# Sparse attention of a two-model kernel: seven program blocks turned into one pipeline over pairs of heads

## The reference, cut to what matters

```python
s_c = einsum('bqgrd,bngd->bgrqn', q_blk, ck) * scale      # 15 compressed blocks
p_c = softmax(where(valid_c, s_c, NEG_INF)) * valid_c
o_c = einsum('bgrqn,bngd->bqgrd', p_c, cv)
...                                                       # o_s: chosen blocks, o_w: window of 512
out = g[..., 0:1] * o_c + g[..., 1:2] * o_s + g[..., 2:3] * o_w
```

## Time and profile before

| | us |
|---|---|
| median of 3 runs | 2824.45 (2823.25 to 2824.95) |
| the profiled execution | 2822.43 |
| its span | 2820.7 |
| TensorE, VectorE, ScalarE, GpSimd busy | 2485.3, 1855.9, 1334.9, 204.7 |
| mean granted TensorE clock, share of full | 0.91 |
| of it from `nsa`'s start to its end (1713.0 to 1849.4) | 136.4, granted clock 0.51 |

### The profile page before, as it was taken

How to read it: one execution, slowest core, us unless ns; L and a number is a source line. 1 busy time by engine, 2 the same in 40 slices (tenths; PEclk the granted TensorE clock), 3 DMA queues, 4 the chain that set the end, 5 groups by cost and what they waited for, 6 DMA issues and landing times. The chain is left out here.

```text
span 2820.7 us, 45360 instructions
## 1 busy us (share of the span) xinstructions
PE 2485.3 (88%) x17186; PEld 2233.7 (79%) x17186; DVE 1855.9 (66%) x3132; ACT 1334.9 (47%) x2140; POOL 204.7 (7%) x181
## 2 busy tenths in 40 slices
PE   7888999899978899795389985937899999999998
PEld 5877897789877789794389974626899999999997
DVE  3645555555564555656755552665899999999897
ACT  2343433443344344422144431303677777777776
POOL 0500000000013000071000032000000000000000
PEclk9999999999989999895589985558999999999999
DMA  8604554445531345340045440002799999999995
GB/s 322 253 16 182 214 215 151 165 174 215 194 107 44 132 172 191 126 150 0 0 150 187 172 169 15 1 0 83 287 344 328 342 343 327 341 343 333 329 344 219
DMA packets 82041, 541.75 MB, mean 192 GB/s; under 512 B 9328, under 2 KB 9776, under 8 KB 33840
## 3 DMA queue, kind: packets, MB, share of 16 engines
q1 hardware_dynamic: 79184, 529.57, 50.9%
q10 hardware_dynamic: 2656, 9.40, 0.9%
HBM read 537.88 MB, written 1.05 MB: 191 GB/s over the span
## 5 line engine op out<-in xcount | busy, mean ns | idle before, releaser
L843 PE MATMUL bank<-w_hi,src_hi 128*128 128x256 f32 x2304 | 671.8, 292 | 15.3 <-DVE src_lo L614 4.4
L2471 DVE TENSOR_TENSOR w_lo<-ring,w_hi 128x1024 fp32r<-128x1024 f32 x528 | 637.7, 1221 | 61.3 <-ACT w_hi L2407 41.8
L844 PE MATMUL bank<-w_lo,src_hi 128*128 128x256 f32 x2304 | 653.1, 283 | 0.0
L845 PE MATMUL bank<-w_hi,src_lo 128*128 128x256 f32 x2304 | 652.3, 283 | 0.0
L843 PEld LDWEIGHTS bank<-w_hi,src_hi 128*128 128x128 f32 x2304 | 441.3, 192 | 39.2 <-issue 30.4
L844 PEld LDWEIGHTS bank<-w_lo,src_hi 128*128 128x128 f32 x2304 | 442.0, 192 | 12.1 <-issue 6.7
L845 PEld LDWEIGHTS bank<-w_hi,src_lo 128*128 128x128 f32 x2304 | 442.1, 192 | 0.0
L843 PE MATMUL bank<-src_hi,w_hi 128*128 128x256 f32 x1472 | 426.8, 290 | 12.7 <-DVE w_lo L1150 8.9
L1150 DVE TENSOR_TENSOR w_lo<-ring,w_hi 128x1024 fp32r<-128x1024 f32 x264 | 322.8, 1223 | 169.5 <-ACT w_hi L1087 169.3
L844 PE MATMUL bank<-src_lo,w_hi 128*128 128x256 f32 x1472 | 421.9, 287 | 0.0
L845 PE MATMUL bank<-src_hi,w_lo 128*128 128x256 f32 x1472 | 421.5, 286 | 0.0
(11 more groups left out here) (349 smaller groups left out, 3076.5 us busy)
## 6 DMA issues: line engine op xcount, KB each, us to landing
ring<-in_moe SPq DMA_DIRECT2D x176, 1024.0 KB, 7.2
ring<-in_ffn SPq DMA_DIRECT2D x66, 1536.0 KB, 6.5
ring<-in_moe SPq DMA_DIRECT2D x176, 512.0 KB, 6.8
ring<-in_ffn_ev SPq DMA_DIRECT2D x22, 1536.0 KB, 6.6
oT<-in_w_ada SPq DMA_DIRECT2D x20, 1024.0 KB, 5.4
big<-in_w_ada SPq DMA_DIRECT2D x20, 1024.0 KB, 8.4
ring<-in_w_in SPq DMA_DIRECT2D x18, 1024.0 KB, 6.3
ring<-in_w_out SPq DMA_DIRECT2D x12, 1024.0 KB, 4.9
```

The source lines that it names most:

```text
L843: pe.matmul(out, ah, bh, start=start and i == 0, stop=False, skip_group_check=True)
L844: pe.matmul(out, ah, bl, start=False, stop=False, skip_group_check=True)
L845: mm = pe.matmul(out, al, bh, start=False, stop=stop and i == n - 1, skip_group_check=True)
L2471: dve.tensor_tensor(wl, piece, wh.bitcast(F32), ALU.subtract).then_inc(p.w_lo[kind].sem, 1)
```

## The change

`nsa_compress` goes, and `nsa` becomes a single block with one list for each engine. The helpers `turn`, `attention`, `head_norm` are no longer used there.

- Heads are reordered on the host (0, 4, 1, 5, ...), so that 128 neighbouring columns hold one head of each group. A transpose of 128x128 then gives a pair, and keys and values of both groups lie on both halves of the partitions too. `w1`, `w2` and the position columns are stored twice, on partitions 0 to 63 and 64 to 127.
- Compression: each group has its own half of the array's rows and of its output partitions: 64 products of 64x64 with 64x15 for each kind.
- Eight units: pair m (0 to 3), branch w (0 or 1). A unit holds both heads and both token tiles: 384 key columns a head. GpSimd builds the values with a column of ones. Gates are multiplied into the inverse sums.
- The compressed branch is laid as steps between the units (`compressed_step`): block-diagonal keys and values give all heads' scores in 8 products and the output of a token tile in one of 128x512.

```diff
-def nsa_compress(p, w1, w2):
...
-    turn(p, heads_to_T(proj, 0, 8, to(qT, 0)) + heads_to_T(proj, 768, 2, to(kT, 0))
-         + heads_to_T(proj, 1024, 2, to(kT, 2)))
...
-    attention(p, items)
...
+    units = [(w, m) for m in range(4) for w in range(2)]
+    nu = len(units)
+    AT = (0, P, 3 * P)
+    jobs = [("c", 0, 512), ("c", 1, 640), ("k", 0, 768), ("q", 0, 0), ("k", 1, 1024), ("q", 1, P), ("q", 2, 2 * P),
+            ("q", 3, 3 * P)]
+    by_act = (0, 1, 3, 5, 7)
...
+        @block.gpsimd
+        def _(pool):
+            for w in range(2):
+                for b in range(2):
+                    a = 896 + 256 * w
+                    pool.tensor_copy(v1[:, b, w, :, 0:HD], proj[:, b, a:a + P].rearrange("p (g d) -> p g d", g=2)
+                                     ).then_inc(v_kept.sem, 1)
...
+            rsqrts(p, pool, [2], parts=N_CMP)
...
+            def turn_job(j):
+                if j >= 4:
+                    pe.wait_ge(*job_kept(j - 4))
+                for t in range(NT):
+                    a = jobs[j][2]
+                    mm = pe.transpose(p.ps[4 + j % 4][:, t * P:t * P + P], proj[:, t, a:a + P], p.ident[:, :])
...
+            def hidden(kind):
+                pe.wait_ge(*posed(2 * kind + 2))
+                for i in range(32):
+                    for g in range(2):
+                        r = slice(g * HD, g * HD + HD)
+                        mm = pe.matmul(p.ps[2 * kind + g][r, 0:N_CMP], w1[kind][r, i, :], flat[r, kind, i, :],
+                                       start=i == 0, stop=i == 31)
...
+            def score(u):
...
+                if u >= 2:
+                    pe.wait_ge(*probs(4 * (u - 1)))
+                else:
+                    pe.wait_ge(*kept(2 * u + 2))
+                for t in range(NT):
+                    for h in range(2):
+                        r = slice(h * HD, h * HD + HD)
+                        mm = pe.matmul(p.ps[2 * (u % 2) + h][:, AT[t]:AT[t + 1]], qT[r, m, t * P:t * P + P],
+                                       kT[r, w, 0:(t + 1) * P], start=True, stop=True)
...
+            def turn_probs(u):
+                for h in range(2):
+                    pe.wait_ge(*probs(4 * u + 2 * h + 2))
+                    if u:
+                        pe.wait_ge(*pt_kept(2 * u + h - 1))
+                    for b in range(3):
+                        mm = pe.transpose(p.ps[4 + h][:, b * P:b * P + P], E[:, u % 2, h, b * P:b * P + P], p.ident[:, :])
...
+            def values(u):
...
+                    pe.wait_ge(*done(u))
+                for h in range(2):
+                    pe.wait_ge(*pt_kept(2 * u + h + 1))
+                    for t in range(NT):
+                        for b in range(t + 1):
+                            a = AT[t] + b * P
+                            mm = pe.matmul(pv_out()[:, h, t, :], PT[:, u % 2, h, a:a + P], v1[:, b, w, h, :],
+                                           start=b == 0, stop=b == t)
...
+            def compressed_step(u):
+                if u == 3:
...
+                if u == 5:
+                    pe.wait_ge(*placed(1))
+                    for t in range(NT):
+                        for m in range(4):
+                            a = (t * 4 + m) * 32
+                            mm = pe.matmul(bank[:, a:a + 32], qT[:, m, t * P:t * P + P], ckbd, start=True, stop=True)
...
+                if u == 9:
+                    pe.wait_ge(*c_kept(1))
+                    for t in range(NT):
+                        if t:
+                            pe.wait_ge(*c_taken(t))
+                        pe.matmul(bank, PTc[:, t * P:t * P + P], Vbd.rearrange("p m g d -> p (m g d)"), start=True,
+                                  stop=True).then_inc(c_out.sem, 1)
...
+            for j in range(4):
+                turn_job(j)
+            hidden(0)
+            for j in range(4, 8):
+                turn_job(j)
+            hidden(1)
+            compressed(0)
+            compressed(1)
+            for u in range(nu + 2):
+                if u < nu:
+                    score(u)
+                if 1 <= u <= nu:
+                    turn_probs(u - 1)
+                if u >= 2:
+                    values(u - 2)
+                compressed_step(u)
...
+            for u in range(nu + 1):
+                if u >= 1:
+                    keep_probs(u - 1)
+                if u < nu:
+                    exps(u)
...
+            def maxima(u):
+                st = stat(u)
+                dve.wait_ge(*scores(u + 1))
+                s = p.psum[:, 2 * (u % 2):2 * (u % 2) + 2, 0:3 * P]
+                edge = p.con_at(CON2, "causal", NT)[:, 0, 0:P].unsqueeze(1).broadcast_to([P, 2, P])
+                dve.tensor_tensor(s[:, :, 0:P], s[:, :, 0:P], edge, ALU.add)
+                chain(dve.tensor_tensor(s[:, :, 2 * P:3 * P], s[:, :, 2 * P:3 * P], edge, ALU.add))
+                for t in range(NT):
+                    ins = dve.tensor_reduce(st[:, 2 * t:2 * t + 2], s[:, :, AT[t]:AT[t + 1]], AX_X, ALU.max)
+                chain(ins)
+                dve.tensor_scalar(st[:, 0:4], st[:, 0:4], -scale, None, ALU.mult).then_inc(negmax.sem, 1)
...
+            def keep(u):
...
+                chain(dve.reciprocal(r.unsqueeze(3), o[:, :, :, HD:HD + 1]))
+                chain(dve.tensor_tensor(r, r, gx[:, :, 2 * m:2 * m + 2, 1 + w].rearrange("p t h -> p h t"), ALU.mult))
+                wide = r.unsqueeze(3).broadcast_to([P, 2, NT, HD])
+                if w == 0:
+                    dve.tensor_tensor(out_rows(m), o[:, :, :, 0:HD], wide, ALU.mult).then_inc(done.sem, 1)
+                else:
+                    dve.tensor_tensor(tmp, o[:, :, :, 0:HD], wide, ALU.mult).then_inc(done.sem, 1)
+                    dve.wait_ge(*done(u + 1))
+                    chain(dve.tensor_tensor(out_rows(m), out_rows(m), tmp, ALU.add))
...
+            for u in range(nu + 2):
+                if u < nu:
+                    maxima(u)
+                if u >= 2:
+                    keep(u - 2)
+                compressed_step(u)
```

More of the change, by code:

```diff
@@ new lines, in job_kept, with job_dst, stat, pv_out @@
+    def job_kept(j):
+        if j in by_act:
+            return kept_a(1 + by_act.index(j))
+        return kept_v(1 + [i for i in range(len(jobs)) if i not in by_act].index(j))
+    def job_dst(j):
+        kind, i, a = jobs[j]
+        return {"c": cT, "k": kT, "q": qT}[kind][:, i, :]
+    def stat(u):
+        return p.att[:, u % 4, :]
+    def pv_out():
+        return p.ps[6][:, 0:260].rearrange("p (h t d) -> p h t d", h=2, t=NT)
+    def out_rows(m):
+        return proj[:, :, m * P:m * P + P].rearrange("p t (h d) -> p h t d", h=2)
@@ L2025, in _, with keep_turned, keep_probs @@
         @block.scalar
         def _(act):
[L2027 removed]
+            def keep_turned(j):
+                act.wait_ge(*turned(j + 1))
+                act.activation(job_dst(j), p.ps[4 + j % 4][:, 0:T], ACT.Copy).then_inc(kept_a.sem, 1)
+            def keep_probs(u):
+                if u >= 2:
+                    act.wait_ge(*pv(u - 1))
+                for h in range(2):
+                    act.wait_ge(*pt_ready(2 * u + h + 1))
+                    act.activation(PT[:, u % 2, h, :], p.ps[4 + h][:, 0:3 * P], ACT.Copy).then_inc(pt_kept.sem, 1)
@@ new lines, in exps, with hidden_exp @@
+            def exps(u):
+                st = stat(u)
+                act.wait_ge(*negmax(u + 1))
+                for h in range(2):
+                    for t in range(NT):
+                        act.activation(E[:, u % 2, h, AT[t]:AT[t + 1]], p.ps[2 * (u % 2) + h][:, AT[t]:AT[t + 1]], ACT.Exp,
+                                       bias=st[:, 2 * t + h:2 * t + h + 1], scale=scale).then_inc(probs.sem, 1)
+            def hidden_exp(kind):
+                for g in range(2):
+                    r = slice(g * HD, g * HD + HD)
+                    act.wait_ge(*hid(2 * kind + g + 1))
+                    if kind:
+                        act.wait_ge(*act_done(g + 1))
+                    act.activation(hsb[r, 0, :], p.ps[2 * kind + g][r, 0:N_CMP], ACT.Exp, scale=-1.0).then_inc(act_exp.sem, 1)
@@ L2042, in nsa, with keep_turned, pose @@
-    gate_exp.passed(1)
+            keys = ck[:, 0, :, :]
+            def keep_turned(j):
+                dve.wait_ge(*turned(j + 1))
+                dve.tensor_copy(job_dst(j), p.ps[4 + j % 4][:, 0:T]).then_inc(kept_v.sem, 1)
+            def pose(kind):
+                dve.wait_ge(*job_kept(kind))
+                pos = p.col("cmp_pos", kind, 32)
+                for half in range(2):
+                    src = cT[:, kind, 16 * half:16 * half + 16 * N_CMP].rearrange("p (n i) -> p i n", i=16)
+                    dve.tensor_tensor(flat[:, kind, 16 * half:16 * half + 16, :], src,
+                                      pos[:, 16 * half:16 * half + 16].unsqueeze(2).broadcast_to([P, 16, N_CMP]),
+                                      ALU.add).then_inc(posed.sem, 1)
@@ new lines, in activate @@
+            def activate(kind):
```

(9 more changed lines are left out.)

301 lines of the change are left out of this document (187 added, 114 removed).

## The result

The changed kernel takes **2757.07 us**, median of four runs (2755.51 to 2760.07), beside 2824.7 us for the kernel before on the same chip: ratio 0.9762, interval 0.9746 to 0.9779. A second measurement of the unchanged file gave 2757.34 us and 0.9769 (0.9752 to 0.9785). The forecast was 2757. The total agrees closely, but its parts do not, and the parts are what the rest of this text is about.

A forecast was written before the change was run, and what follows sets the result against it. The stage, 135.9 us run one after another at the low clock, was taken to lie wholly on the path. Front 11.3 plus pipeline 56.3 saved 67.6 us: 2754.8, or 2757 on the median's scale; range 2746 to 2777.

The forecast's parts named there:

- The sign named for the doubled loads: Weight loads doubled to 1 MB each, priced at nothing; a stage start later than 1713.6 would mean they reach the projection.
- Front: Stage start to first scores: transposes, compression and hidden matmuls end at 23.8 us instead of 35.1, saving 11.3 us.
- round of hidden: Compression's hidden matmuls for one kind, 128 instructions over two groups: 7.0 us taken, between 5 side by side and 10 serial.
- Pipeline: Eight units with compressed steps: fill to 13.6 us, units 3 to 7 23.4, drain 7.5; 44.5 us against 100.8.
- 2T > 6.0 + 1.1: Pipelined loop: waits between engines bound the period T of a unit, so T = 3.6 us, or 3.5 plus VectorE's compressed step.
- VectorE's floor of 36.4 us: Pipelined loop: VectorE's own work, 27.3 us for eight units plus 9.1 us of compressed steps.
- from unit 3 on: Pipelined loop: TensorE's clock assumed at the upper level, 2.4 GHz, from unit 3.
- What this stage loses the span loses: Whole stage: it is wholly on the path and mla waits only for it, so all 67.6 us saved leave the span.
- Half clock: Pipelined loop: clock stays at 0.50 or falls in units 6 and 7, TensorE binds; +14, 2771 us, chance 0.22.
- quadrants in series: Front: hidden matmuls on the quadrants run one after another, 10 us a kind; +6, 2763 us, chance 0.09.
- a serial pipeline: Loop: an unseen wait serialises each unit, 7 to 8.5 us; units 3 to 7 cost 16 more, 2773 us, chance 0.06.
- Slower than before: Front: alternating quadrants cannot be pipelined, each hidden instruction costs full latency, plus a drain per switch; 2835 us, chance 0.01.

The follow-up runs named there:

- without the mask: The changed kernel with the two causal mask additions of each maxima on VectorE left out: 2751.1 us, ratio 0.9750.
- quadrants by group: The changed kernel with each group's hidden matmuls run in turn on one 64x64 quadrant, then the other, instead of alternating: 2774.9 us, ratio 0.9833.
- values first: The changed kernel with two banks for the final compressed products, and TensorE doing values(u-2) ahead of turn_probs(u-1): 2759.2 us, ratio 0.9774.
- the products ahead of the front: The changed kernel with 15 unused 128x512 products on TensorE behind the projection's last chunk: 2763.0 us, ratio 0.9792.
- the not pipelined version: The changed kernel with each engine doing all of unit u before unit u+1: 2798.3 us, ratio 0.9917.

## Why the prediction was right, and where not

- **The bound and the lever: right.** The stage lay wholly on the path, no weights moved, and its engines waited for each other. Undoing the pipeline alone gives back 41 of 67 us. The sign named for the doubled loads, a stage start later than 1713.6, did appear (1716.3) but has another cause: the whole program is already 2.6 us later some 300 us earlier (a step of GpSimd starts at 1410.18 against 1407.57 us), long ahead of these loads, and the slower load lands 9.0 us after its issue in place of 7.6.
- **Front, forecast 23.8 us, measured 22.6.** The 7.0 us for a round of hidden is exact by luck: I took the row of the old matmul between 5 and 10, without a reason. An instruction on one quadrant costs 0.105 us at 15 moving columns and 0.109 at 30, and alternation halves it. The step "One after another they cost half more than now" is wrong: they cost 13.4 us, nearly double. Had the quadrants not alternated, the rival's 2763 would have been off by 12 us.
- **Pipeline, forecast 44.5 us, measured 40.7 (38.0 with the drain at the full clock).** Fill 10.5 in place of 13.6, since the clock rose already in unit 2. Units 3 to 7 20.5 in place of 23.4: the step that failed is the latency, "2T > 6.0 + 1.1", which would allow no unit under 3.55 us; unit 3 took 3.26, and 2.61 without the mask. In those 20.5 us VectorE is busy 18.4 and TensorE 18.2, and VectorE's waits for values are nearly gone. The two engines together bind, not the loop of waits, and neither alone: "VectorE now has more to do than TensorE" makes too much of one of them, since taking 3.0 us of its work away gave 1.0. VectorE's floor of 36.4 us was too high as well: it is busy 30.5 us of the 40.7. The drain took 9.8 us against 7.5, at the low clock; 7.0 where it stayed high.
- **The clock "from unit 3 on": right in the change, and closer than 0.22 for the rival says.** Three edits (quadrants by group, values first, the products ahead of the front) had units of 5 to 6.5 us at 1.2 GHz. The Trainium skill's rule on psum-queue cycling ("TensorE: Matmul & The Clock Gate") tells of swings between both levels in a kernel whose TensorE idles briefly between groups. The change's own loop shows none from 1749 to 1770 us. Two variants show a dip, but in windows in which TensorE is busy 3.00 of 3 us, so the rule's condition isn't what these runs show.
- **"What this stage loses the span loses": wrong.** This is the step that failed most. The stage lost 72.6 and 75.4 us in its two profiles, 5.0 and 7.8 more than the 67.6 summed, and the span 62.4 and 64.9. mla gave back 5.1 and 6.2 us, in its attention, where the clock was low. What was priced at nothing, mla, unedited, takes 69.2 to 69.3 us or 74.0 to 75.4, and in the one profile of the kernel before it had the short time; the short one stood in two of the ten later profiles that leave mla alone. So the change meets the long one more often than not. Whether the kernel before nearly always has the short one isn't known from one profile, nor is what decides between them. The rest, 2.7 us at the stage's start and 2.4 behind the routing, lies within what these stretches vary by.
- So that 2757 came out right to 0.1 us is luck: a saving in the stage that was summed too small met a give-back that was not in the sum.
- **Rivals.** Half clock, quadrants in series, a serial pipeline: none happened in the change, but for the drain, which ran at 1.2 GHz in one of its two profiles and cost 2.8 us. Each was produced by an edit. Of the prices only that of a unit at the low clock was about right (6.1 us, measured 5 to 6.5); the serial pipeline was priced at 16 us and cost 41. Slower than before: the not pipelined version, the worst of these, is still at 0.9917.

## What to carry to other kernels

When a saving is worked out for a stage, look at the TensorE-light stretch that follows it: at the same instructions it may have two durations, here 7 to 9% apart, one with the granted clock up and one with it low, and a single profile of the kernel before shows only one of them. In a software pipeline near balance, price the second engine as well as the first before shortening the first: here 3 us of VectorE's work were worth 1. Small products on one quadrant took about the same time with 15 columns as with 30, so alternate the quadrants (and with them the banks, as here).

## What was not expected of the hardware

- A 64x64 product costs about the same at 1.2 GHz with 15 moving columns (0.105 us) as with 30 (0.109), and half that (0.055) when the next goes to the other quadrant and bank.
- The granted clock fell in windows in which TensorE is busy 3.00 of 3 us (1759 us in two variants), and stayed at 0.50 through 20.2 busy us of 22.6 in the front. A busy TensorE in the profile doesn't keep the clock up by itself.
- Behind the same 22.2 us of idle TensorE and the same 26 transposes, the clock stayed up through mla's attention in some profiles (0.99 in the kernel before) and fell back in others (0.69 in the change).
- With unused products up to 0.42 us ahead of the transposes the clock was 1.00 over 25 us and 0.95 over the 21.7 behind; with products that ended 5.1 us ahead it was 0.57 in the attention. Ahead of the front, it was 1.00 for the first transposes and 0.50 in the quadrant products that followed 1.2 us of waiting.
